# Hybrid decoder step on one core: the middle of the input projections issued in another order

## The reference

```python
cols = x @ lp['w_in']
y_a = attn(q, k, v, qi, ki, wi)          # sparse attention, keys chosen by an indexer
y_b = rwkv7_mix(cols[B_START:B_END])     # RWKV-7 state update
y_c = gated_short_conv(cols[C_START:C_END])
y_d = rglru_block(cols[D_START:D_END])   # short convolution, gated linear recurrence
mix = concat([y_a, y_b, y_c, y_d]) @ lp['w_out']
x = layer_norm(ALPHA * x + mix)
x = layer_norm(ALPHA * x + moe(x))       # 16 experts, two per token
```

## Time and profile before

| | us |
|---|---|
| median of 3 runs | 1359.83 (1358.13 to 1360.35) |
| profiled execution | 1366.04 |
| its span, first to last instruction | 1364.4 |
| TensorE busy in the span | 1148.9 (84%) |
| VectorE busy | 649.8 (48%) |
| ScalarE busy | 329.4 (24%) |
| GpSimd busy | 160.2 (12%) |
| mean granted clock of TensorE | 0.908 |

### The profile page before, as it was taken

The page is one execution under the profiler, slowest core; times in us unless marked ns, Lnnn a source line. Parts: engine busy times, 40 slices in busy tenths (PEclk is TensorE's granted clock), DMA queues, the critical chain, the costliest instruction groups (busy, mean ns, idle before and its releaser), DMA issues.

```text
span 1364.4 us, 24557 instructions
## 1 busy us (share of the span) xinstructions
PE 1148.9 (84%) x9786; PEld 699.0 (51%) x9786; DVE 649.8 (48%) x1353; ACT 329.4 (24%) x774; POOL 160.2 (12%) x225
## 2 busy tenths in 40 slices
PE   4989999997789829999499799999878991999940
PEld 2466878894354513333146667789735451333310
DVE  0035699687724430111463358988764434111128
ACT  1044224120532102111133342323034210111110
POOL 0050003502200020000200100061050002000020
PEclk9997999898799859999899889999889995999985
DMA  7079211002862376997720212110085518699832
GB/s 279 9 292 408 80 62 31 21 5 66 261 235 109 163 299 248 416 426 285 259 99 21 81 32 71 54 32 7 3 254 201 215 69 333 228 399 423 328 138 105
DMA packets 66468, 240.37 MB, mean 176 GB/s; under 512 B 8530, under 2 KB 29170, under 8 KB 56818
## 3 DMA queue, kind: packets, MB, share of 16 engines
q1 hardware_dynamic: 47872, 172.97, 33.7%
q0 software_dynamic: 14592, 52.10, 10.5%
q10 hardware_dynamic: 3890, 13.72, 2.5%
HBM read 190.21 MB, written 50.78 MB: 177 GB/s over the span
## 4 chain that ended last, share of the span: by engine, by line
PE 73%; DVE 10%; ACT 4%; DMA 3%; issue 3%; DVEq 2%; SPq 2%; POOL 1%; POOLq 0%; ACTq 0%
PE ps L748 14%; PE ps L1287 12%; PE ps L881 11%; PE ps L1244 8%; PE ps L728 8%; PE ps L1302 6%; SPq L482 2%; PE ps L1274 2%; PE ps L1116 1%; PE ps L807 1%; ACT arena L1380 1%; DMA arena<-in_wa 1%; DVE arena L1925 1%; DVE arena L2285 1%; POOL rows_in L659 1%
## 5 line engine op out<-in xcount | busy, mean ns | idle before, releaser
L1380 ACT ACTIVATE arena<-ps 128x512 f32<-128x512 f32 (+14 forms) x342 | 142.6, 454 | 653.6 <-PE ps L748 158.6
L748 PE MATMUL ps<-arena 128*128 128x272 f32 x1088 | 262.2, 401 | 0.0
L748 PEld LDWEIGHTS ps<-arena 128*128 128x128 f32 x1088 | 209.6, 194 | 51.0 <-issue 5.5
L1287 PE MATMUL ps<-arena 128*32 128x512 f32 x1536 | 169.7, 592 | 4.8 <-ACT arena L1380 4.8
L881 PE MATMUL ps<-arena 64*64 64x64 f32 (+3 forms) x4016 | 155.5, 238 | 14.1 <-DVE arena L2142 10.3
L881 PEld LDWEIGHTS ps<-arena 64*64 64x64 f32 x4016 | 141.0, 139 | 27.7 <-issue 16.2
L728 PE MATMUL ps<-arena 128*128 128x512 f32 (+1 forms) x256 | 106.7, 578 | 22.0 <-DMA arena<-in_wa 18.5
L1244 PE MATMUL ps<-arena 128*128 128x512 f32 x256 | 114.1, 601 | 0.0
L1287 PEld LDWEIGHTS ps<-arena 128*32 128x32 f32 x1536 | 51.2, 109 | 117.0 <-issue 117.0
L1302 PE MATMUL ps<-arena 128*32 128x512 f32 x768 | 87.4, 595 | 3.3 <-DVE arena L2600 2.0
L728 PEld LDWEIGHTS ps<-arena 128*128 128x128 f32 x256 | 50.0, 198 | 74.6 <-issue 74.5
(11 more groups left out here) (346 smaller groups left out, 1304.0 us busy)
## 6 DMA issues: line engine op xcount, KB each, us to landing
arena<-in_w_gu SPq DMA_DIRECT2D x32, 2048.0 KB, 13.8
arena<-in_w_dn SPq DMA_DIRECT2D x32, 1024.0 KB, 14.2
arena<-in_wf SPq DMA_DIRECT2D x34, 512.0 KB, 3.6
rows_in<-arena POOLq DMA_DIRECT2D x12, 1024.0 KB, 24.2
arena<-rows_in SPq DMA_DIRECT2D x24, 512.0 KB, 13.8
rows_out<-arena ACTq DMA_DIRECT2D x24, 512.0 KB, 8.7
arena<-in_cache_v POOLq DMA_DIRECT2D x64, 128.0 KB, 5.7
arena<-in_cache_k SPq DMA_DIRECT2D x64, 128.0 KB, 5.5
```

The costliest lines, as they stand in the source:

```text
L748: mm = pe.matmul(ps[:, 2 + 2 * h + n % 2, 0:HALF], m.wf[n % 3][:, c, :], m.xT[:, c, h * HALF:h * HALF + HALF], start=c == 0, stop=c == KC - 1)
L1287: mm = pe.matmul(ps[q, 3 + k, :], m.xgT[:, c, q], m.w_gu[HOME[i]][:, c, :], start=c == 0, stop=c == KC - 1, skip_group_check=True)
L1380: return act.activation(out, in_, ACT.Copy)
```

## The change

Three queues get another order in the middle of the projections. On TensorE the first three transposes are now the indexer's query and key and the first half of q, the others come behind chunk 8; a column chunk stands between any two users of banks 6, 7, 0 and 1; the indexer's turns come ahead of the low-rank products, which are split in two pairs; the sample scores come ahead of turn 2. ScalarE's calls follow in the same order, the tanh and sigmoid of chunk 0 go ahead of chunk 1's copies, and the gate square waits for `rw_in`. VectorE does the decays, key rates, bonus and block queries later, begins the selection with one round of the first chain alone and one of chains 0 and 3, does both convolutions ahead of `key_norms` and `chunk_inputs`, and the rounds that are left (two chains or three in two of them) behind. The number of rounds of each chain in the projections stays ten. Waits are fitted to the new order.

```diff
     def head_transposes(l, first):
         pe.wait_ge(s["kr_ready"], nth(l, "kr_ready", 1))
-        srcs = [m.A[:, :, 128 * k:128 * k + 128] for k in range(4)] + [m.A[:, :, C_QI:C_QI + 128], m.KR]
+        srcs = [m.A[:, :, C_QI:C_QI + 128], m.KR] + [m.A[:, :, 128 * k:128 * k + 128] for k in range(4)]
+        if first:
+            pe.wait_ge(s["job_out"], nth(l, "job_out", 4))
         for b in range(first, first + 3):
-            if b >= 3:
-                pe.wait_ge(s["tr_copied"], nth(l, "tr_copied", b - 2))
-                pe.wait_ge(s["tr_sample"], nth(l, "tr_sample", 1))
...
     def indexer(l, i):
         if i < 3:
             pe.wait_ge(s["relu_done"], nth(l, "relu_done", 4 * (3 - i)))
         else:
-            pe.wait_ge(s["job_out"], nth(l, "job_out", 4))
+            pe.wait_ge(s["s_relu"], nth(l, "s_relu", 1))
         for h in range(4):
+            if i == 2 and h == 2:
+                pe.wait_ge(s["s_score"], nth(l, "s_score", 1))
...
     def sample_scores(l):
-        pe.wait_ge(s["relu_done"], nth(l, "relu_done", 12))
+        pe.wait_ge(s["relu_done"], nth(l, "relu_done", 4))
...
-    def loras(l):
+    def lora(l, a):
         pe.wait_ge(s["lora_act"], nth(l, "lora_act", 1))
-        pe.wait_ge(s["s_relu"], nth(l, "s_relu", 1))
-        for a, rows in enumerate((slice(0, 32), slice(32, 64))):
-            for p in range(2):
-                product(l, 2 * a + p, m.param("lora")[rows, 128 * p:128 * p + 128], m.Z[rows, 6, :])
+        pe.wait_ge(s["relu_done"], nth(l, "relu_done", 12))
+        rows = slice(32 * a, 32 * a + 32)
+        for p in range(2):
+            product(l, 2 * a + p, m.param("lora")[rows, 128 * p:128 * p + 128], m.Z[rows, 6, :])
     def key_norms(l):
         pe.wait_ge(s["kk_in"], nth(l, "kk_in", 1))
-        pe.wait_ge(s["s_score"], nth(l, "s_score", 1))
+        pe.wait_ge(s["tr_copied"], nth(l, "tr_copied", 6))
+        pe.wait_ge(s["tr_sample"], nth(l, "tr_sample", 2))
...
     def projections(l):
...
         columns(l, 0, 1)
         head_transposes(l, 0)
-        head_transposes(l, 3)
         columns(l, 2)
         sample_indexer(l)
-        loras(l)
+        columns(l, 3)
         indexer(l, 3)
-        columns(l, 3)
+        columns(l, 4)
+        sample_scores(l)
         indexer(l, 2)
-        columns(l, 4)
+        columns(l, 5)
         indexer(l, 1)
-        columns(l, 5)
-        sample_scores(l)
-        columns(l, 6, 7)
+        columns(l, 6)
+        lora(l, 0)
+        columns(l, 7)
+        lora(l, 1)
         columns(l, 8)
+        head_transposes(l, 3)
+        columns(l, 9)
         key_norms(l)
-        columns(l, 9)
+        columns(l, 10)
         bonuses(l)
-        columns(l, 10, 11)
+        columns(l, 11)
         lru_gates(l)
         columns(l, 12, 13, 14, 15, 16)
...
     def projections(l):
...
         for p in range(2):
             job(l, 10 + p, m.za[:, p, :], ACT.Sigmoid, T, m.param("gab")[:, p:p + 1])
         act.drain()
+        act.wait_ge(s["rw_in"], nth(l, "rw_in", 1))
         act.activation(m.gelu, m.gb, ACT.Square, scale=0.044715 ** 0.5).then_inc(s["gate_sq"], 1)
...
     def columns(l):
...
         mix(l, 0, 1)
         split_queries(l)
         mix(l, 2)
         key_squares(l)
         sample_sums(l)
-        decays(l)
+        mix(l, 3)
         scores(l, 3)
-        key_rates(l)
-        mix(l, 3)
+        select_rounds(1, 0)
+        mix(l, 4)
         scores(l, 2)
-        mix(l, 4)
+        start_selection(l)
+        select_rounds(1, 0, 3)
+        mix(l, 5)
         scores(l, 1)
-        bonus(l)
-        mix(l, 5)
-        block_queries(l)
-        start_selection(l)
         select_rounds(1)
         mix(l, 6)
-        select_rounds(3)
+        decays(l)
+        select_rounds(1)
+        key_rates(l)
+        bonus(l)
         conv_d(l, 0)
+        block_queries(l)
+        select_rounds(1)
+        conv_d(l, 1)
         key_norms(l)
         chunk_inputs(l)
-        conv_d(l, 1)
-        select_rounds(4)
+        select_rounds(3)
+        select_rounds(1, 1, 2, 3)
+        select_rounds(1, 1, 2)
         lru_decay(l)
         select_rounds(1)
         lru_input(l)
...
     def split_queries(l):
-        dve.wait_ge(s["tr_sample"], nth(l, "tr_sample", 2))
+        dve.wait_ge(s["tr_sample"], nth(l, "tr_sample", 1))
...
     def block_queries(l):
+        dve.wait_ge(s["tr_sample"], nth(l, "tr_sample", 2))
```

More of the change, by code:

```diff
@@ L1397, in projections @@
         act.activation(m.kist[1], m.kist[1], ACT.Sqrt, bias=m.const("eps")[:, 0:1], scale=1.0 / 32).then_inc(s["ki_std"], 1)
-        columns(l, 0, 1)
+        columns(l, 0)
         act.wait_ge(s["fm_used"], nth(l, "fm_used", 1))
@@ L1401, in projections @@
         act.activation(m.Z[64:128, 6, :], m.Z[64:128, 6, :], ACT.Sigmoid).then_inc(s["lora_act"], 1)
+        columns(l, 1)
         head_columns(l, 0)
-        head_columns(l, 3)
         columns(l, 2)
         sample_indexer(l)
+        columns(l, 3)
+        relus(l, 3)
+        columns(l, 4)
+        sample_scores(l)
+        relus(l, 2)
+        columns(l, 5)
+        relus(l, 1)
+        columns(l, 6)
         for p in range(2):
             job(l, p, m.ea[:, p, :], ACT.Sigmoid, TP, m.param("w0")[:, p:p + 1])
+        columns(l, 7)
         for p in range(2):
             job(l, 2 + p, m.aa[:, p, :], ACT.Sigmoid, TP, m.param("a0")[:, p:p + 1])
-        relus(l, 3)
         act.wait_ge(s["cum_ready"], nth(l, "cum_ready", 1))
@@ L1414, in projections @@
         act.activation(m.en, m.en, ACT.Exp, scale=DECAY).then_inc(s["exps_ready"], 1)
[L1415 to L1421, removed]
         columns(l, 8)
+        head_columns(l, 3)
+        columns(l, 9)
         for p in range(2):
             job(l, 4 + p, m.bv[:, p, :], ACT.Sqrt, TP)
-        columns(l, 9)
+        columns(l, 10)
         for p in range(2):
             job(l, 6 + p, m.bonus[:, p, :], ACT.Copy, T)
-        columns(l, 10, 11)
+        columns(l, 11)
         for p in range(2):
@@ L1583, in head_columns @@
             act.wait_ge(s["x_kept"], nth(l, "x_kept", 0))
-        dst = [m.qT[:, 0, :], m.qT[:, 1, :], m.kT[:, 0, :], m.kT[:, 1, :], m.qiT, m.kiT]
+        dst = [m.qiT, m.kiT, m.qT[:, 0, :], m.qT[:, 1, :], m.kT[:, 0, :], m.kT[:, 1, :]]
         for b in range(first, first + 3):
             act.wait_ge(s["tr_mm"], nth(l, "tr_mm", b + 1))
-            act.activation(dst[b][:, 0:SEQ], ps[:, (6, 7, 0)[b % 3], :], ACT.Copy, scale=0.125 if b < 2 else 1.0)\
+            act.activation(dst[b][:, 0:SEQ], ps[:, (6, 7, 0)[b % 3], :], ACT.Copy, scale=0.125 if b in (2, 3) else 1.0)\
                 .then_inc(s["tr_copied"], 1)
         for b in range(first, first + 3):
-            ins = act.activation(dst[b][:, SEQ:T], ps[:, 1, NS * b:NS * b + NS], ACT.Copy, scale=0.125 if b < 2 else 1.0)
+            ins = act.activation(dst[b][:, SEQ:T], ps[:, 1, NS * b:NS * b + NS], ACT.Copy, scale=0.125 if b in (2, 3) else 1.0)
         ins.then_inc(s["tr_sample"], 1)
@@ L1992, in columns, with select_rounds @@
         rounds = iter(range(17))
-        def select_rounds(n):
+        def select_rounds(n, *chains):
             for _ in range(n):
-                selection_round(next(rounds))
+                selection_round(next(rounds) if not chains else 0, chains or (0, 1, 2, 3))
         mix(l, 0, 1)
@@ L2272, in start_selection, with selection_round @@
         dve.wait_ge(s["s_score"], nth(l, "s_score", 1))
-    def selection_round(r):
-        chains = [(c, rows) for c, (rows, topk) in enumerate(CHAINS) if 8 * r < topk]
+    def selection_round(r, some=(0, 1, 2, 3)):
+        chains = [(c, rows) for c, (rows, topk) in enumerate(CHAINS) if 8 * r < topk and c in some]
         for c, rows in chains:
```

## The result

The changed kernel takes 1339.46 us (median of three runs; 1336.41 to 1344.16) beside 1359.32 us for the kernel before (four runs, 1358.13 to 1360.35): a ratio of 0.9853, 95% interval 0.9825 to 0.988. Run again on another occasion the kernel took 1340.37, ratio 0.9803 (0.9771 to 0.9835). So it is faster by 1.5 to 2%, some 20 to 24 us; 36.5 had been forecast. Both medians, 1339.46 and 1341.81, lie above the range of 1316 to 1339, the first by 0.5 us.

What follows compares the result with a forecast made beforehand. TensorE was taken to set the length, through waits and slow matmuls. Gains of 18.8 + 16.5 + 2.9 - 1.7 = 36.5 us bring 1366.04 to 1329.5 profiled, less 6.2 for the median: 1323.3, range 1316 to 1339.

Steps and rivals of the forecast that it cites:

- I take 18.06: Start of the RWKV stage: GpSimd's first convolution takes 18.06 us (bounds 14.31 and 22.52), leaving a wait of 0.9.
- The rule built on it: Start of the RWKV stage: the convolution delays nothing up to some 20.4 us, and above that one for one.
- rival B: Tail before the RWKV stage: convolution takes 22.52 in both layers, wait 3.0, slow RWKV beginning; 26.5 gained, 1333.3; chance 0.22.
- 227.2 summed: VectorE's end before the RWKV stage, layer 0: 227.2, against TensorE's first product at 229.9; costed at nothing.
- 1.5 taken: Indexer turn 2: an added TensorE wait for ScalarE's copy of the sample scores, 1.5 us lost (bounds nothing or 2.86).
- The 2.9 behind the stage: First 1872 RWKV matmuls, layer 0: with a wait of 0.9 they go as in layer 1, 2.9 us gained.
- the offset of 6.2: Whole kernel: run median taken as 6.2 us below the profiled execution, as before, so 1329.5 becomes 1323.3.
- The three long waits have one cause: TensorE's waits of 5.53, 1.44 and 0.98: shared PSUM banks not yet emptied by ScalarE; 7.95 us gained.
- one fall in two behind the sample indexer: Behind the sample indexer's small matmuls: TensorE's clock falls in one of two layers, 1.7 us lost (bounds 0 and 3.4).
- 1.0 in the gate products: Recurrence's gate products: third product waits about 1.0 for ScalarE's sigmoid table, the wait of 1.22 goes; 0.2 gained.
- the slower rival: ScalarE's gate square: late chunk inputs hold chunk 12's copies and chunk 14; at 225, 6 lost per layer, 1372; chance 0.05.
- rival A: The forecast itself: 1317 to 1328; low end without clock fall or added wait, 41 gained; chance 0.60.

Runs made afterwards that it cites:

- early signal: Changed kernel, but GpSimd's first convolution signals its first source free behind its tail's copy, not behind its last two products: 1331.01 us, ratio 0.9751.
- steps ahead: Changed kernel, but VectorE's two gate steps (lru_decay, lru_input) stand ahead of the selection rounds that preceded them: 1333.81 us, ratio 0.9765.
- tanh back: Changed kernel, but ScalarE's tanh and sigmoid are back behind chunk 1's copies while the transposes stay apart: 1339.52 us, ratio 0.985.
- all four: Changed kernel with early signal, steps ahead, the sigmoid table loaded before chunk 11's copies and the sample scores' copy before chunk 4's: 1325.94 us, ratio 0.9748.

## Why the prediction was wrong

The direction, the place and most of the mechanism were right; the size was not. On the profiled executions 36.5 us were forecast and 1364.4 - 1342.5 = 21.9 came:

| part | forecast | measured | missing |
|---|---|---|---|
| two stages (18.8 + 16.5 - 1.7) | 33.6 | 13.1 + 12.8 = 25.9 | 7.7 |
| first 1872 RWKV matmuls (by windows, as in the earlier trace rows; the timeline reads 0.2 more) | 2.9 | 64.60 to 64.22, 61.69 to 61.86: 0.2 | 2.7 |
| the rest of the span | 0 | -4.2 | 4.2 |

To these 14.6 come 1.5 of the step from profile to median (6.2 forecast, 1344.16 - 1339.46 = 4.7 measured): 16.1 together, which is 1339.5 - 1323.3 but for rounding.

**The step that failed** is "I take 18.06, because VectorE's last recurrence step falls mostly behind it now". The convolution took 23.20 and 22.85, above even the upper bound of 22.52. All the gate steps and the scan fell beside it, and it matters which GpSimd instruction each one meets: 18.06 and 22.52 of before are two such meetings (the scan began at 907.12 in layer 1, as the convolution ended, and at 238.88 in layer 0, in its midst), and neither was a law of the order. The rule built on it (nothing up to 20.4, one for one above) was right, with 20.5. So rival B occurred, at its place and in its parts: 2.7 and 2.3 us in the waits, and the slow start of the RWKV stage in layer 0. Shown by the early signal and by the steps ahead.

**A sum under that step was short too.** VectorE ended at 233.3 in layer 0 for the 227.2 summed. Its idle time from the first mix on fell by 11.2 us (43.7 to 32.5), not by 15.8, and its busy time rose by 1.5. Rival B had named this way to the same tail. How much of the meeting comes from it no run separates; the steps ahead only show that gate steps which begin at 196.31 and 207.92, for 211.00 and 219.11, no longer stretch these products and taps.

**A smaller term was left out.** A chunk between two other users takes 7.6, not its share of a longer run: 7.64 x 3 for 22.28 (0.64), 7.59 + 7.62 for 14.98 (0.23), and chunks 2 and 3 at 7.64 for the 7.42 assumed (0.44): 1.3 in each layer. The added wait of the sample scores (0.85 for the 1.5 taken) gave back 0.6. 2.7 + 1.3 - 0.6 = 3.4 of the 4.0 us missing in layer 0, 2.3 + 1.3 - 0.6 = 3.0 of the 3.7 in layer 1. The 0.6 and 0.7 that are left were not followed.

**The 2.9 behind the stage was one execution's.** It was read off the 64.60 of one profile. In the second profile of before the timeline has 61.90 for the same matmuls, where the first had 64.78, behind a wait of 2.84 for 2.86. So the slow start was not a fixed price of the wait.

**Outside the stages** nothing was forecast and 4.2 were lost, and the offset of 6.2 was carried over. Both are within the scatter of the rest of the span (1014 to 1029 us over twelve profiles), which is too wide to rule out a small cost of the order there. Where the clock falls in it, and why, was not followed.

**A cause was misread, without harm to the sum.** "The three long waits have one cause" is wrong of the first: 4.0 of its 5.53 us were ScalarE's tanh and sigmoid. The sum was unharmed because the chunk put between hides the one as well as the other (tanh back).

**Right:** the waits that went, and the slow matmuls behind them; one fall in two behind the sample indexer; 1.0 in the gate products (1.03). The gate square was not held: the chunk inputs were there at 191.4, ScalarE at 193.8, a margin of 2.4 us that had been put at 3, so the slower rival was never near. VectorE did not set the end; its slack was right (3.86 for "some 3") by luck, because TensorE was late too. The one fall in two is no law either: the steps ahead and all four had slow third chunks in both layers, the early signal in none. With the tail alone mended (early signal), the stages are 156.18, a fall of 1.7 in it, and 154.50, where 153.1 had been forecast without a fall: the 1.4 more are the 1.3 left out, less the 0.6, and the 0.7 not followed. The 1325.94 of all four is no test of the forecast, since two waits are gone there that it had priced as staying (1.5 and 1.0). One slip has no part in this: rival A's low end, 41 gained, gives 1318.6 and not 1317.

## What to carry to other kernels

The transfer of buffers from GpSimd to ScalarE had a threshold here, some 20.5 us. Look for one in other such transfers: work out how long the producer may take before anybody waits, and then price the whole spread of its durations in the profile, not the one that suits the argument. Here the new order even went beyond that spread. If a buffer's last read is not the last instruction of a function, signal it there; here that alone was worth some 9 us.

Before a wait is put down to an order of TensorE, read what the engine it waits for was doing in it. Two table loads and two activations behind the wrong copy had been 4 us of a wait that looked like a matter of PSUM banks.

If a kernel's stages repeat within 1 us and its total scatters by 10, compare stages.

## What the runs showed of the hardware

- GpSimd and VectorE in turns: a 128x32 product of 0.26 us took 1.30 beside a VectorE instruction with two tensor inputs, a 128x512 tap of 1.57 took 3.53 beside two of them, and VectorE's own 1.29 became 2.37. Selection rounds beside the same GpSimd instructions cost nothing (1.28, 0.25 and 1.57 us in the steps ahead).
- GpSimd paused once behind its first small instruction after 114 to 134 us without work: 2.23 us in layer 0, 1.86 in layer 1, in all twelve profiles, and not in the second convolution, which follows within 6 us. What it does then the profile does not show.
- A wait of about 3 us ahead of the RWKV stage cost between 0 and 2.9 more behind it: its first 1872 matmuls take 61.90 us at a clock of 1.00 and took, behind waits of 2.8 to 3.8, from 61.90 to 64.78. Behind 0.89 they took 61.9 to 62.1 wherever VectorE kept up. The same wait thus cost its length or up to twice that, and how much changed from layer to layer and from profile to profile.
